# The first expert pair of a mixture-of-experts layer takes the form of the other three

## The chip, the cores and the metric

The kernel runs on one core of one Trainium2 chip, in one launch. The metric is the device time of that launch in microseconds (us); the median of a few runs counts. The profile is of one execution of its own, whose span is given beside it.

## The reference, cut to what matters

The program is one step of a small language model: an attention layer with a dense feed-forward part, then a state-space layer with a mixture of experts. There are 264 tokens, 256 of a prompt and 8 of samples. Only the last part, the mixture of experts, is touched:

```python
def moe(h, w_router, w_gate, w_up, w_down):
    probs = jax.nn.softmax((h @ w_router).astype(F32), axis=-1)
    top_p, top_i = lax.top_k(probs, TOP_K)              # TOP_K = 2 of N_EXPERTS = 8
    top_p = top_p / jnp.sum(top_p, axis=-1, keepdims=True)
    combine = jnp.sum(jax.nn.one_hot(top_i, N_EXPERTS, dtype=F32) * top_p[..., None], axis=-2)
    y = 0
    for e in range(N_EXPERTS):
        y = y + combine[..., e:e + 1] * swiglu(h, w_gate[e], w_up[e], w_down[e])
    return y
```

D_MODEL is 1024, an expert's hidden width is 2816, everything is float32. `setup_inputs(seed=0)` draws the inputs. Where the reference's own router is evaluated on these default inputs, the 528 choices of its 264 tokens fall on experts 0 to 7 like this: 104, 58, 93, 35, 49, 65, 69, 55.

## The kernel before

**Experts by pairs.** The router's counts are sorted on VectorE, but expert 0 is always put at rank 0 (its key gets 1e6 added), so that its weights can be fetched before the router has decided. Ranks 1 to 7 follow by falling count. Pair p joins the expert of rank p ("heavy") with that of rank 4+p ("light"). Each pair has a fixed room for tokens, whatever the counts are: pair 0 has 128 tokens of expert 0 (`CAPH`) and 64 of its light expert (`CAPL`), pairs 1 to 3 have 96 (`CAP2`) and 64.

**Rounds.** The whole of the four pairs stands in a loop `Fori(0, rounds)` on each engine, and each round reads all weights of all eight experts again. `rounds` is computed on the chip (lines 2438 to 2448): it is 1 if count 0 less 32 (`CAPH - CAP2`), count 1, and count 4 plus 32 (`CAP2 - CAPL`) are at most 96, else 2, or 3 for still greater ones (the numbers are ranks). Tokens beyond the room are taken in the next round.

**Pair 0** has a form of its own. Its columns are cut into `GROUPS` of 512 (the last of 256), and `first_steps()` sets the order: the heavy expert's gate, up and down products of a group with 128 tokens as one 128x128 load and 512 moving columns (lines 1515 and 1556), the light ones, a step behind, with 64 tokens in two column groups of the array (lines 1530 and 1568). Its heavy tokens are gathered by products with a 0/1 matrix `pick` (line 1424), its light ones and all of pair 1 by an indirect DMA from a copy `hrow` of the tokens in memory, turned on TensorE (lines 1433, 1451, 1452).

**Pairs 1 to 3** run `pair_gate_up`, `pair_turn` and `pair_down` over three `SUPER` groups of 1024, 1024 and 768 columns. Four 32-column groups of the array work side by side: three with the heavy expert's 96 tokens and one with 32 of the light ones (lines 1622 and 1672), then the light expert's other 32 tokens (lines 1634 and 1678). While pair p ends, `gather` brings pair p+1's tokens by products (line 1455), and `indices` its row numbers (line 1466).

**Weights** come in tiles of 1 MiB (768 KiB in the last SUPER group) through a ring of 12 slots (`MS`), all issued by SyncE (SP) in the order `MOE_TILES`. A slot is filled again when TensorE has counted `moe_used` up to its tile. The first 10 tiles (`AHEAD`), all of expert 0, are issued before the router is done; the rest from the loop (line 674). At the end of a round SP issues those first tiles again for a next round, each in `PIECES` = 8 pieces of 128 KiB through a small loop (line 680), or in 2 pieces only if no round follows (`piece_step`).

**End of a round.** `return_rows` adds the last pair's rows to the tokens by products (lines 1477 and 1483), `keep_rows` stores the sums on VectorE (line 2566). The first product of a next round (`gather_by_product`) waits for all of `keep_rows`.

Of the kernel before, what the change touches and what calls it, by code (L numbers as in the profile page):

```python
# [13 lines left out]
F32 = mybir.dt.float32  # L14
# [34 lines left out]
ROUNDS = -(-T // CAPH)  # L49
# [15 lines left out]
GROUPS = [(512 * g, min(512, FF - 512 * g)) for g in range(-(-FF // 512))]  # L65
NG = len(GROUPS)
GATHERS = 5 + 4 * (NP - 1)
ROWS_IN = 48
# [4 lines left out]
EVENTS = 2 * NG + 9 * (NP - 1)  # L73
COPIES = 2 * NG + 2 * NSG * (NP - 1)


FIRST = 8
RETURNS = (2, 0, 1)
KEPT = 7


def first_steps():


    return [(g if g < NG else None, g - 1 if g >= 1 else None) for g in range(NG + 1)]


def first_events():


    return [(who, g) for hg_, lg in first_steps() for who, g in (("heavy", hg_), ("light", lg)) if g is not None]


def moe_order():


    def gate_up(who, g):
        return [(0, who, kind, g, i) for kind in ("gate", "up") for i in range(GROUPS[g][1] // 256)]

    def down(who, g):  # L100
        return [(0, who, "down", g, i) for i in range(GROUPS[g][1] // 256)]

    order = []
    for hg_, lg in first_steps():
        if hg_ is not None:
            order += gate_up("heavy", hg_)
        if lg is not None:
            order += down("heavy", lg)
        if lg:
            order += down("light", lg - 1)  # L110
        if lg is not None:
            order += gate_up("light", lg)
    order += down("light", NG - 1)
# [16 lines left out]
AHEAD, PIECES = 10, 8  # L130
# [15 lines left out]
def moe_round(t):  # L146


    return 16 * (MT // MS) + (16 * (PIECES - 1) if t % MS < AHEAD else 0)
# [42 lines left out]
def build(nc, a, o):  # L192
# [5 lines left out]
    def sem(name):  # L198
# [154 lines left out]
    actH, sgH = actX[:, 0:512], actX[:, 512:D]  # L353
# [22 lines left out]
    twice = sb("twice", [P, 2, CAPL], c=c4)  # L376
# [3 lines left out]
    actL, sgL = actLx[:, 0:256], actLx[:, 256:512]  # L380
# [3 lines left out]
    turnL = turnB[:, :, :].rearrange("p (q u) t -> p q (u t)", q=2)  # L384
# [3 lines left out]
    hrow = nc.dram_tensor("hrow", [T, D], F32, kind="Internal").ap()  # L388
    hgrow = sb("hgrow", [P, 2, D], c=c4)
    rowix = [sb(f"rowix{i}", [P, 1], I32, c=c4) for i in range(2)]  # L390
# [5 lines left out]
    xs2 = hgrow[0:NB, 0, :]  # L396
# [27 lines left out]
      gathered index_done index_ready rows_out rows_gathered hg_ready ye_ready rows_added gates_copied moe_used  # L424
# [22 lines left out]
    first_packed = {kind: a[f"moe_first_{kind}"] for kind in ("gate", "up", "down")}  # L447
    md = a["moe_w_down"].rearrange("e (c p) n -> e p c n", p=P)
# [61 lines left out]
    def index_bank(p):  # L510

        return bank[7] if p < 2 else bank[0]
# [11 lines left out]
    def _(sp):  # L524
# [76 lines left out]
        def first_tile(tile):  # L601


            _, _, kind, g, i = tile
            f0, width = GROUPS[g]
            base = f0 * D + i * P * SLOT
            return first_packed[kind][base:base + P * SLOT].rearrange("(p n) -> p n", p=P)

        def packed_rows(kind, e, g, block):
# [4 lines left out]
            return packed[kind][ds(e - 1, 1), base:base + P * rows * width].rearrange("a (p c n) -> (a p) c n", p=P, c=rows)  # L614

        def moe_load(tile, e):

            p, who, kind, g, i = tile
            t = MOE_AT[tile]
            f0, width = SUPER[g] if p else GROUPS[g]  # L620
            if not p and who == "heavy":
                src = first_tile(tile)
                dst = moe_slot(t)[:, 0:src.shape[1]]
            elif kind == "down" and p:
                src = md_rows[ds(e - 1, 1), :, f0 // 256 + i, :].rearrange("a p n -> (a p) n")
                dst = moe_slot(t)
            elif kind == "down":
                c0_ = f0 // P + 2 * i
                src = md[ds(e - 1, 1), :, c0_:c0_ + 2, :].rearrange("a p c n -> (a p) c n")
                dst = moe_slot(t).rearrange("p (c n) -> p c n", c=2)  # L630
            elif p:
                src = packed_rows(kind, e, g, i // (PACK[g] // 2))
                src = src[:, i % (PACK[g] // 2) * 2:i % (PACK[g] // 2) * 2 + 2, :].rearrange("p c n -> p (c n)")
                dst = moe_slot(t)[:, 0:2 * width]
            else:
                rows = SLOT // width
                G0 = SUPER[g // 2][0]
                src = packed_rows(kind, e, g // 2, i // (PACK[g // 2] // rows))
                c0_ = i % (PACK[g // 2] // rows) * rows
                src = src[:, c0_:c0_ + rows, f0 - G0:f0 - G0 + width]  # L640
                dst = moe_slot(t).rearrange("p (c n) -> p c n", c=rows)
            sp.dma_start(dst, src).then_inc(moe_ready[t % MS], 16)

        def moe_piece(t, j):


            src = first_tile(MOE_TILES[t])
# [15 lines left out]
        sp.wait_ge(s["router_done"], 1)  # L663
        for t in range(FIRST, AHEAD):
            moe_load(MOE_TILES[t], 0)
        sp.wait_ge(s["router_done"], 5)
        rounds = sp.value_load(rnd[0:1, 0:1], min_val=1, max_val=ROUNDS)
        with sp.Fori(0, rounds) as r:
            for p in range(NP):
                expert = pair_ids(p)  # L670
                for tile in tiles_of(p):
                    if MOE_AT[tile] >= AHEAD:
                        sp.wait_ge(s["moe_used"], r * MT + (MOE_AT[tile] + 1))
# [16 lines left out]
    def _(g):  # L690
# [124 lines left out]
        def gather_rows(who, cap):  # L815
            g.indirect_dma_start(out=hgrow[0:cap, who, :], out_offset=None, in_=hrow[:, :],
                                 in_offset=bass.IndirectOffsetOnAxis(ap=rowix[who][0:cap, 0:1], axis=0)).then_inc(s["rows_gathered"], 16)

# [4 lines left out]
        with g.Fori(0, rounds) as r:  # L823
            for p in range(NP):
                n = r * NP + p
                if p == 0:
                    g.wait_ge(s["index_ready"], 2 * n + 2)
                    log(5 * n)
                    gather_rows(1, CAPL)
                if p < NP - 1:  # L830
                    g.wait_ge(s["index_ready"], 2 * n + 4)
                    log(5 * n + 1)
                    if p == 0:
                        gather_rows(0, P)
                        gather_rows(1, CAPL - CAPA)
# [3 lines left out]
                    add_rows(xrow[:, :], addix[p % 2][0], yeH, CAP2 if p else CAPH)  # L839
# [12 lines left out]
    def _(pe):  # L852
# [561 lines left out]
        def gather_by_product(r):  # L1414
# [1346 lines left out]
```

## Time and profile before

| what | us |
|---|---|
| median of 3 runs | 1588.38 |
| lowest, highest | 1583.31, 1594.08 |
| the profiled execution: time | 1581.58 |
| the profiled execution: span | 1580.0 |

The span is shown on the page in 40 slices of 39.5 us, with the busy share of each engine in tenths. TensorE (PE) is busy in nearly all of them. The share of the 16 DMA engines is 9 in the first slice and then again from slice 25 on, to the end: these are the experts' weights. The clock granted to TensorE is 0.978 of full speed over the whole span. A matmul of float32 stands in the records as two, so that a count of records is twice the count of products in the code. Times in the views count from the start of the span. "PEld" is the load of the stationary operand, "SPq" the queue of SyncE that issues DMAs.

### The profile page before, as it was taken

How to read it: one execution, taken by the hardware profiler on the slowest of the kernel's cores; microseconds unless marked ns; L12 is line 12 of the kernel's file. 1: busy time of each engine (PE TensorE's matmuls, PEld its weight loads, DVE VectorE, ACT ScalarE, POOL GpSimd, SP SyncE). 2: the span in 40 equal slices, each digit the busy share in tenths (PEclk: the TensorE clock that was granted, in tenths of full speed). 3: DMA queues.
4: the chain of work that ended last, by engine and by line, in shares of the span. 5: the costliest groups of instructions: out<-in, count | busy, mean ns of one | idle time of the engine just before them, and what ended most of it. 6: DMA issues, size and time to landing. Idle time of an engine off the chain costs nothing.

```text
span 1580.0 us, 24287 instructions
## 1 busy us (share of the span) xinstructions
PE 1494.8 (95%) x9928; PEld 885.9 (56%) x9928; DVE 370.3 (23%) x903; ACT 260.1 (16%) x586; POOL 111.2 (7%) x167
## 2 busy tenths in 40 slices
PE   6999877999999999999998999999999999998998
PEld 3544545788888878778785554553344234432342
DVE  2223431300000055634576100001000100011104
ACT  2122320200000022357503100000000000000001
POOL 1101550000000000000010100000000100010000
PEclk9999997999999999999999999999999999999999
DMA  9759987244334553472358899999999999999995
GB/s 379 306 214 392 365 289 240 107 162 160 122 105 146 197 189 120 155 263 94 147 211 349 288 348 379 392 408 401 421 417 419 405 420 417 420 404 419 418 418 220
DMA packets 104011, 463.22 MB, mean 293 GB/s; under 512 B 16110, under 2 KB 35339, under 8 KB 62261
## 3 DMA queue, kind: packets, MB, share of 16 engines
q1 hardware_dynamic: 91136, 420.49, 68.7%
q0 software_dynamic: 10256, 39.98, 7.3%
q8 instruction: 79, 1.29, 0.3%
q10 hardware_dynamic: 2512, 1.23, 0.3%
q14 instruction: 28, 0.23, 0.0%
HBM read 446.30 MB, written 15.55 MB: 292 GB/s over the span
## 4 chain that ended last, share of the span: by engine, by line
PE 76%; DMA 11%; DVE 5%; issue 4%; POOL 2%; ACT 1%; SPq 0%; POOLq 0%; DVEq 0%
PE bank L1622 11%; PE bank L1177 10%; PE bank L1147 8%; PE bank L1672 5%; PE bank L1191 5%; PE bank L1515 5%; DMA ring<-in_moe_w_up 4%; DMA ringx<-in_moe_w_up 3%; PE bank L1634 3%; PE bank L1225 3%; PE bank L1530 2%; PE bank L1556 2%; PE bank L890 2%; PE bank L924 2%; PE bank L977 2%
## 5 line engine op out<-in xcount | busy, mean ns | idle before, releaser
L1622 PE MATMUL bank<-ring,hg 128*32 128x512 f32 (+1 forms) x1456 | 208.5, 566 | 7.8 <-DMA ring<-in_moe_w_up 7.1
L1177 PE MATMUL bank<-hT,ring 128*128 128x264 f32 x704 | 156.9, 386 | 0.3 <-ACT hT L1725 0.3
L1622 PE MATMUL bank<-ringx,hg 128*32 128x512 f32 (+1 forms) x848 | 146.1, 568 | 3.8 <-DMA ring<-in_moe_w_up 2.8
L1177 PEld LDWEIGHTS bank<-hT,ring 128*128 128x128 f32 x704 | 133.7, 190 | 23.4 <-issue 0.6
L1622 PEld LDWEIGHTS bank<-ring,hg 128*32 128x32 f32 x1456 | 62.7, 111 | 110.3 <-issue 99.8
L1147 PE MATMUL bank<-hT,ring 128*128 128x264 f32 x512 | 118.7, 394 | 1.7 <-ACT hT L1725 1.3
L1147 PEld LDWEIGHTS bank<-hT,ring 128*128 128x128 f32 x512 | 99.1, 194 | 19.9 <-issue 2.1
L1672 PE MATMUL bank<-ring,turnH 128*32 128x512 f32 x768 | 92.6, 603 | 0.0
L1191 PE MATMUL bank<-actT,ring 128*128 128x264 f32 x352 | 79.1, 386 | 0.6 <-DVE actT L2210 0.6
L1515 PE MATMUL bank<-ring,hg 128*128 128x512 f32 (+1 forms) x192 | 78.0, 560 | 0.6 <-ACT hg L1940 0.6
L1622 PEld LDWEIGHTS bank<-ringx,hg 128*32 128x32 f32 x848 | 44.2, 112 | 59.6 <-issue 55.8
L1191 PEld LDWEIGHTS bank<-actT,ring 128*128 128x128 f32 x352 | 66.8, 190 | 12.4 <-DVE actT L2210 1.0
L2628 DVE TENSOR_TENSOR actX<-actX,bank 128x512 f32<-128x512 f32 (+1 forms) x18 | 10.8, 640 | 265.3 <-PE bank L1622 265.3
L1147 PE MATMUL bank<-sz,ring 128*128 128x264 f32 x256 | 60.1, 394 | 3.9 <-DVE sz L2367 3.9
L1225 PE MATMUL bank<-hT,ring 128*128 128x264 f32 x256 | 60.0, 390 | 0.0
L1147 PEld LDWEIGHTS bank<-sz,ring 128*128 128x128 f32 x256 | 49.6, 194 | 13.2 <-DVE sz L2367 4.3
L1672 PEld LDWEIGHTS bank<-ring,turnH 128*32 128x32 f32 x768 | 26.3, 111 | 54.7 <-issue 54.5
L1515 PEld LDWEIGHTS bank<-ring,hg 128*128 128x128 f32 x192 | 35.6, 190 | 36.7 <-issue 35.9
L1225 PEld LDWEIGHTS bank<-hT,ring 128*128 128x128 f32 x256 | 47.6, 190 | 8.9 <-issue 0.9
L1970 ACT ACTIVATE actX<-bank 128x512 f32<-128x512 f32 (+1 forms) x18 | 9.1, 559 | 263.6 <-PE bank L1622 263.6
L890 PE MATMUL bank<-ring,scT 128*32 128x512 f32 x384 | 50.6, 619 | 0.0
L813 POOL DMA_DIRECT2D index_log<-rnd x11 | 6.0, 548 | 545.1 <-DVE yeH L2526 290.4
(565 smaller groups left out, 1787.4 us busy)
## 6 DMA issues: line engine op xcount, KB each, us to landing
ring<-in_moe_w_down SPq DMA_DIRECT2D x53, 1024.0 KB, 17.1
ring<-in_w_ada SPq DMA_DIRECT2D x48, 1024.0 KB, 11.2
ring<-in_moe_w_up SPq DMA_DIRECT2D x40, 1024.0 KB, 16.1
ring<-in_moe_w_gate SPq DMA_DIRECT2D x32, 1024.0 KB, 17.0
ringx<-in_moe_w_gate SPq DMA_DIRECT2D x27, 1024.0 KB, 12.8
ringx<-in_moe_w_down SPq DMA_DIRECT2D x24, 1024.0 KB, 18.1
ring<-in_ssm_w_in SPq DMA_DIRECT2D x20, 1024.0 KB, 4.9
ringx<-in_moe_w_up SPq DMA_DIRECT2D x19, 1024.0 KB, 15.9
```

Source lines behind the costliest of these rows:

```text
L890: m = mm(b_[32 * v_:32 * v_ + 32, :], scT[:, k, :], ring[:, n % NS, 512 * v_:512 * (v_ + 1)], start=k == 0, stop=k == DC - 1, skip_group_c ...
L924: m = mm(out, slot8(n)[:, k, (m_ % 2) * P:(m_ % 2) * P + width], hT[:, k, :], start=k == 0, stop=k == DC - 1)
L977: m = mm(bank[h % 2][0:QK, 0:T], wqb[:, k, h * QK:(h + 1) * QK], projT[:, k, :], start=k == 0, stop=k == QC - 1)
L1147: m = mm(bank[n % 4][:, 0:T], w[:, k, (n % per_tile) * P:(n % per_tile + 1) * P], rhs[:, k, :], start=k == 0, stop=k == kc - 1)
L1177: m = mm(bank[2 * w + q][:, 0:T], slot8(tl)[:, k, q * P:(q + 1) * P], hT[:, k, :], start=k == 0, stop=k == DC - 1)
L1191: m = mm(bank[2 * (j % 2) + q][:, 0:T], slot8(tl)[:, kk, q * P:(q + 1) * P], actT[:, k0 + kk, :], start=k == 0 and kk == 0, stop=k == 3 an ...
L1225: m = mm(bank[n % 2][:, 0:T], slot8(tl)[:, k, (n % 2) * P:(n % 2 + 1) * P], hT[:, k, :], start=k == 0, stop=k == DC - 1)
L1515: m = mm(bank[kind == "up"][:, 0:width], hg[:, k, 0:CAPH], w[:, kk, :], start=k == 0, stop=k == DC - 1)
L1530: m = mm(bank[2][64 * v_:64 * v_ + 64, 256 * b_:256 * b_ + width // 2], hg[:, k, CAPH:CAPS], w[:, kk, v_], start=k == 0, stop=k == DC - 1, ...
L1622: m = mm(bank[2 * b_ + u][rows, 0:HALVES[g][u]], hg[:, k, rows], w[:, kk, 512 * u:512 * u + HALVES[g][u]], start=k == 0, stop=k == DC - 1, ...
L1634: m = mm(bank[7][32 * v_:32 * v_ + 32, 0:half], hg[:, k, CAPH:CAPH + CAPA], light[("gate", "up")[v_ // 2]][:, kk, 512 * (v_ % 2):512 * (v_ ...
L1672: m = mm(bank[4 + half][rows, :], turnH[:, 4 * u + q, rows], w[:, kk, 512 * half:512 * (half + 1)], start=first and kk == 0, stop=last and ...
```

## The change

Pair 0 runs the same code as the other pairs: 96 tokens of expert 0, three column groups of four, with 32 of its light tokens beside them. `GROUPS`, `first_steps` and everything built on them goes. The room for expert 0 is now `CAP2` = 96, and the rule for `rounds` is changed to that. Light tokens of pair 0 and all of pair 1 are gathered by products: the copy `hrow`, the indirect gathers and the index columns `rowix` go. The order of tiles is heavy gate, heavy up, light gate, light up from the start, so that `AHEAD` becomes the six tiles 0, 1, 4, 5, 8 and 9, and the number of tiles grows from 276 to 280 with the same bytes but for rounding. The weights of all experts are packed alike.

```diff
-ROUNDS = -(-T // CAPH)
+ROUNDS = -(-T // CAP2)
...
-AHEAD, PIECES = 10, 8
+PIECES = 8
+AHEAD = [t for t in range(MS) if MOE_TILES[t][1] == "heavy"]
...
+def slot_free(t):
+    return t + 1 if t >= MT % MS else t + 1 + MS - MT % MS
...
         sp.wait_ge(s["st_ready"], NB - 2)
-        for t in range(FIRST):
-            sp.wait_ge(s["units"], unit(WOUT + t))
+        for t in AHEAD:
+            if t < NS:
+                sp.wait_ge(s["units"], unit(WOUT + t))
+            else:
+                sp.wait_ge(s["router_done"], 1)
             moe_load(MOE_TILES[t], 0)
...
-            for t in range(AHEAD):
-                sp.wait_ge(s["moe_used"], r * MT + (MT + t + 1))
+            for t in AHEAD:
+                sp.wait_ge(s["moe_used"], r * MT + (MT + slot_free(t)))
                 moe_piece(t, 0)
                 with sp.Fori(1, PIECES, step) as j:
                     moe_piece(t, j)
...
-        for t, (t0, tn) in enumerate(TOKS):
-            g.wait_ge(s["rows_copied"], DC + 2 * t + 4)
-            g.dma_start(hrow[t0:t0 + tn, :], htok[0:tn, t, :]).then_inc(s["rows_out"], 16)
-        g.wait_ge(s["rows_out"], 64)
...
-        def gather_by_product(r):
+        def gather_first(r):
             pe.wait_ge(s["rows_kept"], r * KEPT + 1)
...
-                        m = mm(bank[i % 2][:, j * CAPS:j * CAPS + CAPH], htok[0:tn, t, c * P:(c + 1) * P], pick[0:tn, t, 0:CAPH],
+                        m = mm(bank[i % 2][:, j * CAPS:j * CAPS + CAP2], htok[0:tn, t, c * P:(c + 1) * P], pick[0:tn, t, 0:CAP2],
                                start=t == 0, stop=t == 2)
                 m.then_inc(s["gathered"], 1)
+            pe.wait_ge(s["pick_ready"], r * NP + 1)
             for c in range(DC):
-                m = pe.transpose(bank[2][:, c * CAPL:(c + 1) * CAPL], hgrow[0:CAPL, 1, c * P:(c + 1) * P], ident[0:CAPL, 0:CAPL])
+                for t, (t0, tn) in enumerate(TOKS):
+                    m = mm(bank[2][:, c * CAPL:(c + 1) * CAPL], htok[0:tn, t, c * P:(c + 1) * P], pick[0:tn, t, CAP2:CAP2 + CAPL],
+                           start=t == 0, stop=t == 2)
             m.then_inc(s["gathered"], 1)
...
-            gather_by_product(r)
-            pe.wait_ge(s["hg_ready"], r * GATHERS + 4)
-            for step, (hg_, lg) in enumerate(first_steps()):
...
-            for p in range(1, NP):
+            gather_first(r)
+            indices(r * NP, 0)
+
+            for p in range(NP):
                 n = r * NP + p
...
         for i in (1, 2):
-            ins = v.scalar_tensor_tensor(out=cmx[:, i:i + 1], in0=sorted_cnt[:, 0:1], scalar=float(i * (CAP2 - CAPH)), in1=sorted_cnt[:, 1:2],
-                                         op0=ALU.add, op1=ALU.max)
+            ins = v.tensor_tensor(cmx[:, i:i + 1], sorted_cnt[:, 0:1], sorted_cnt[:, 1:2], ALU.max)
         link(ins)
```

The lines behind this, which turn `cmx` into `rounds`, stay as they are:

```python
        for i in (1, 2):
            ins = v.scalar_tensor_tensor(out=cmx[:, i:i + 1], in0=sorted_cnt[:, NP:NP + 1], scalar=float(i * (CAP2 - CAPL)), in1=cmx[:, i:i + 1],
                                         op0=ALU.add, op1=ALU.max)
        link(ins)
        link(v.tensor_scalar(cmx[:, 0:1], cmx[:, 1:2], float(CAP2), 1.0, ALU.is_gt, ALU.add))
        link(v.scalar_tensor_tensor(out=cmx[:, 3:4], in0=cmx[:, 2:3], scalar=float(2 * CAP2), in1=cmx[:, 0:1], op0=ALU.is_gt, op1=ALU.add))
        v.tensor_copy(rnd[:], cmx[0:1, 3:4]).then_inc(s["router_done"], 1)
```

## Rows read from the trace of the kernel before

**Rows 1.** Windows by stage: pair 0, pairs 1 to 3, the end
```profile
core 0: us, PE busy (x) PEld busy (x) DVE busy (x) ACT busy (x) POOL busy (x), PEclk, DMA share, GB/s
869.70:1066.10 196.40, 194.63 (x893) 101.40 (x895) 17.17 (x63) 14.76 (x29) 11.34 (x14) 0.99 0.97 363
1066.10:1230.00 163.90, 162.47 (x1506) 59.84 (x1508) 12.89 (x41) 9.82 (x19) 3.73 (x4) 0.99 1.02 415
1230.00:1397.90 167.90, 162.80 (x1508) 62.33 (x1500) 16.23 (x39) 11.01 (x21) 4.77 (x5) 0.99 1.01 415
1397.90:1561.40 163.50, 153.79 (x1434) 52.81 (x1426) 23.36 (x44) 10.74 (x19) 6.03 (x7) 0.98 1.00 406
1561.40:1580.00 18.60, 11.58 (x50) 4.94 (x46) 11.73 (x17) 5.07 (x15) 0.00 (x0) 0.85 0.22 79
```
**Rows 2.** The page's costliest groups: the products of pairs 1 to 3
```profile
L1622 PE MATMUL bank<-ring,hg 128*32 128x512 f32 (+1 forms) x1456 | 208.5, 566 | 7.8 <-DMA ring<-in_moe_w_up 7.1
L1622 PE MATMUL bank<-ringx,hg 128*32 128x512 f32 (+1 forms) x848 | 146.1, 568 | 3.8 <-DMA ring<-in_moe_w_up 2.8
```
**Rows 3.** Timeline of VectorE where the counts become `rounds` and `pick`
```profile
867.05 0.22 DVE L2437 TENSOR_REDUCE sorted_cnt<-order 128x8 f32<-128x64 f32 x1
867.30 0.23 DVE L2439 SCALAR_TENSOR_TENSOR cmx<-sorted_cnt 128x1 f32<-128x1 f32 x2
868.21 0.14 DVE L2448 CAST rnd<-cmx 1x1 int32<-1x1 f32 x1
871.65 0.67 DVE L2476 TENSOR_SCALAR pick<-twice,slots 128x128 f32<-128x128 f32 x3
```
**Rows 4.** Chain that ended last, start of pair 0: start, us, what
```profile
869.72 8.52 PE bank L1424 x48
878.24 0.02 issue
878.26 0.39 ACT hg L1940
878.65 0.22 issue
878.87 13.99 PE bank L1515 x32
```
**Rows 5.** Timeline of TensorE: a gather at 160 columns, the indices of a later pair
```profile
1198.59 4.89 PE L1455 MATMUL bank<-pick,htok 128*128 128x160 f32 x24
1148.65 1.97 PE L1466 MATMUL bank<-tags,pick 128*96 128x3 f32 x18
```
**Rows 6.** Timeline of SP's queue: last early tiles, first tiles of a light expert
```profile
860.05 1.69 SPq L642 DMA_DIRECT2D ringx<-in_moe_first_down  x2
871.49 1.48 SPq L642 DMA_DIRECT2D ringx<-in_moe_w_gate  x2
```
**Rows 7.** DMA issues: xcount, KB each, median us from issue to landing
```profile
ring<-in_moe_w_down SPq DMA_DIRECT2D x53, 1024.0 KB, 17.1
ring<-in_ssm_w_in SPq DMA_DIRECT2D x20, 1024.0 KB, 4.9
```
**Rows 8.** Windows of 20 us in pair 2, columns as in group 1
```profile
1360.00:1380.00 20.00, 20.00 (x159) 8.68 (x151) 0.29 (x1) 1.47 (x3) 0.00 (x0) 1.00 1.02 422
```
**Rows 9.** Timeline: the last products, the end of `return_rows` and `keep_rows`
```profile
1557.05 3.64 PE L1672 MATMUL bank<-ringx,turnH 128*32 128x512 f32 x32 [0.32 <-DMA ringx<-in_moe_w_down]
1560.48 1.07 PE L1678 MATMUL bank<-ringx,turnB 128*32 128x512 f32 x8
1571.43 1.29 DVE L2566 TENSOR_TENSOR yout<-yout,bank 128x512 f32<-128x512 f32 x2 [0.98 <-PE bank L1483]
```
**Rows 10.** SP's issues in pieces at the round's end, and how they land
```profile
1556.16 2.40 SPq L649 DMA_DIRECT2D ring<-in_moe_first_up  x4
1558.84 2.64 SPq L649 DMA_DIRECT2D ringx<-in_moe_first_down  x4
L649 SPq DMA_DIRECT2D ringx<-in_moe_first_down x4: 347/350/711, 1558.8 to 1561.1; - x4
DMA to landing us min/median/max: 2.8/4.8/19.9
```
**Rows 11.** Bytes read from and written to memory, from the page
```profile
HBM read 446.30 MB, written 15.55 MB: 292 GB/s over the span
```

More of the change, by code:

```diff
@@ L72 @@
 HALVES = [(512, w - 512) for f0, w in SUPER]
-EVENTS = 2 * NG + 9 * (NP - 1)
-COPIES = 2 * NG + 2 * NSG * (NP - 1)
-FIRST = 8
+EVENTS = 9 * NP
+COPIES = 2 * NSG * NP
 RETURNS = (2, 0, 1)
 KEPT = 7
[L82 to L91, printed above, removed]
 def moe_order():
[L97 to L101, printed above, removed]
     order = []
[L104 to L113, printed above, removed]
     def down_pair(p, g):
         return [(p, who, "down", g, i) for i in range(SUPER[g][1] // 256) for who in ("heavy", "light")]
-    for p in range(1, NP):
+    for p in range(NP):
         for g in range(NSG):
@@ L613, in packed_rows, with moe_source @@
             base = f0 * D + block * P * rows * width
-            return packed[kind][ds(e - 1, 1), base:base + P * rows * width].rearrange("a (p c n) -> (a p) c n", p=P, c=rows)
+            return packed[kind][ds(e, 1), base:base + P * rows * width].rearrange("a (p c n) -> (a p) c n", p=P, c=rows)
+        def moe_source(tile, e):
+            _, _, kind, g, i = tile
+            if kind == "down":
+                return md_rows[ds(e, 1), :, SUPER[g][0] // 256 + i, :].rearrange("a p n -> (a p) n")
+            src = packed_rows(kind, e, g, i // (PACK[g] // 2))
+            return src[:, i % (PACK[g] // 2) * 2:i % (PACK[g] // 2) * 2 + 2, :].rearrange("p c n -> p (c n)")
         def moe_load(tile, e):
-            p, who, kind, g, i = tile
             t = MOE_AT[tile]
[L620 to L642, printed above, removed]
+            src = moe_source(tile, e)
+            sp.dma_start(moe_slot(t)[:, 0:src.shape[1]], src).then_inc(moe_ready[t % MS], 16)
         def moe_piece(t, j):
-            src = first_tile(MOE_TILES[t])
+            src = moe_source(MOE_TILES[t], 0)
             w = src.shape[1] // PIECES
@@ L1461, in indices @@
             pe.wait_ge(s["pick_ready"], n + 1)
[L1462 to L1463 removed]
+            for r0, r1, c0_, q in ((0, CAP2, 0, p), (CAP2, P, 0, NP + p), (0, P, 8, NP + p)):
                 for t, (t0, tn) in enumerate(TOKS):
@@ L1548, in heavy_down @@
-            def heavy_down(g):
-                pe.wait_ge(s["moe_copied"], turns_before("heavy", g) + 1)
-                if g == 0:
-                    pe.wait_ge(s["ye_ready"], 3 * n + 2)
-                for i in range(GROUPS[g][1] // 256):
-                    w = weights(0, "heavy", "down", g, i)
-                    for q in range(2):
-                        for half in range(2):
-                            m = mm(bank[4 + half][:, :], turnH[:, 2 * i + q, :], w[:, q, 512 * half:512 * (half + 1)],
-                                   start=g == 0 and i == 0 and q == 0, stop=g == NG - 1 and q == 1)
-                    m.then_inc(s["moe_used"], 1)
@@ L1560, in light_down @@
-            def light_down(g):
-                pe.wait_ge(s["moe_copied"], turns_before("light", g) + 1)
-                if g == 0:
-                    pe.wait_ge(s["ye_ready"], 3 * n + 3)
-                for i in range(GROUPS[g][1] // 256):
-                    w = weights(0, "light", "down", g, i)
-                    for q in range(2):
-                        for v_ in range(2):
-                            m = mm(bank[6][64 * v_:64 * v_ + 64, :], turnL[:, i, 64 * q:64 * q + 64], w[:, q, 512 * v_:512 * (v_ + 1)],
-                                   start=g == 0 and i == 0 and q == 0, stop=g == NG - 1 and q == 1, skip_group_check=True)
-                    m.then_inc(s["moe_used"], 1)
@@ L2496, in row_indices @@
                 v.wait_ge(s["rows_added"], rows_in_memory(r, 1))
-            v.tensor_scalar(rowix[0][:], ix[:, 0:1], -1.0, 0.0, ALU.add, ALU.max)
-            few = CAPA if p else CAPL
-            if p < 2:
-                v.tensor_scalar(rowix[1][0:few, :], ix[0:few, 8:9], -1.0, 0.0, ALU.add, ALU.max)
             ins = v.tensor_copy(slotw[u][:], ix[:, 0:16].rearrange("p (w c) -> p w c", c=8)[:, :, 0:3])
@@ L2520, in heavy_slot_rows @@
         def heavy_slot_rows(r, p):
-            v.wait_ge(s["moe_used"], r * MT + moe_done(p, "heavy", "down", (NSG if p else NG) - 1))
+            v.wait_ge(s["moe_used"], r * MT + moe_done(p, "heavy", "down", NSG - 1))
             v.wait_ge(s["rows_added"], rows_in_memory(r, p))
```

273 lines of the change are left out of this document (56 added, 217 removed).

## The prediction

> **What bounds the kernel now.** I read the windows by stage first [rows 1]. From 869.7 us on, everything is the experts. In pair 0 TensorE is busy 194.6 of 196.4 us while the DMA engines move 363 GB/s: TensorE is the bound. In pairs 1 to 3 both are at their limit: TensorE is busy 162.5 of 163.9, 162.8 of 167.9 and 153.8 of 163.5 us (pair 3 gathers nothing), and the DMA share is 1.00 to 1.02 at 406 to 415 GB/s. So a pair in the wide form costs about 164 us whichever way one looks, and one in the old form 196.
>
> The second thing to read is a count. Line 1622 makes 1152 products in three pairs, which is 2304 records; the page has 1456 + 848 = 2304 [rows 2]. The loop over rounds has run exactly once. This sets what the time is made of: one round is 691.7 us (869.7 to 1561.4) of 1580, so whatever touches the number of rounds outweighs everything else in the diff.
>
> **The rule for rounds.** The counts of the default inputs are 104 for expert 0, and 93, 69, 65, 58, 55, 49, 35 for the others by rank. Before: max(104 - 32, 93, 58 + 32) = 93, not over 96, one round. After: max(104, 93, 58 + 32) = 104, over 96, and max(104, 93, 58 + 64) = 122, not over 192: two rounds. Eight tokens of expert 0 have no room in the first round, and for these the second reads all eight experts again, since no product or load in the loop depends on how many tokens a slot holds.
>
> Did the chip see these inputs? The counts themselves do not stand in a trace; the instructions that sort them take the same 0.22 us whatever they hold [rows 3]. But the single round [rows 2] is a test of them: it needs count 0 up to 128, rank 1 up to 96 and rank 4 up to 64. I evaluated the router on seeds 0 to 5 under both of the random generator's modes: of 12 draws only two pass, the default one and one more (49 tokens for expert 0). That speaks strongly for the default inputs, and the margin of 8 tokens is no matter of rounding.
>
> **The first round's start.** Heavy tokens are still gathered by 24 products, and 24 more now follow for the light ones. At 128 moving columns 48 records took 8.52 us [rows 4]; at 160 columns 24 records took 4.89 us [rows 5]. Going by columns down to 64 would give about 6.5 us, going by the number of products 8.5; I take 8.5 for both parts and keep 2 us each as the bound. The light part's `pick` was ready at 872.3 us [rows 3]; nine VectorE operations in place of three add perhaps 1.5 us, still before TensorE is through the heavy part at 878.2. The indices of pair 0, 18 records at 1.9 us [rows 5], now stand ahead of the first weights, and the copy of the light tokens lies beside them. First expert product: 869.7 + 8.5 + 8.5 + 1.9 = 888.6 us (before 878.9).
>
> Loads: only six tiles can be fetched early, because the light expert isn't known before. SP gets past the router at 871.5 [rows 6]; six tiles of 1.05 MB at 422 GB/s [rows 8] are 15 us, so the ring is full at about 888. This costs nothing; were TensorE ready at 880, it would cost 8 us. The `hrow` copies and gathers that go were beside other work: nothing. Waits taken away on SP, POOL and ACT end no earlier than what follows them.
>
> **The first round's pairs.** By TensorE: 3 x 163.9 + 153.8 = 645.5 us (the first pair now as the second, with a gather for the next). By DMA: eight experts are 8 x 3 x 1024 x 2816 x 4 B = 277 MB; less 12.6 MB in the ring at the start, at 415 GB/s, 637 us, plus the last tiles' products of 4.3 us [rows 9]: 641. As these two are so close, they will take turns in holding the other up, as they did before: the old pairs 1 to 3 took 495.3 us where TensorE alone needs 481.6. From above, the sum of the old pairs with a second "pair 1" is 495.3 + 163.9 = 659.2. I take 652, the middle. The round's products end at 888.6 + 652 = 1540.6 us (before 1561.4): the wide form alone is worth some 21 us.
>
> The Trainium skill's page "DMA: Bandwidth & Descriptors", section "Specifications", gives a fabric ceiling of 435 GB/s and a limit of about 358 GB/s for the memory of one core. The rate of 422 GB/s in a window agrees with the first and not with the second. An estimate by the second would be 774 us for a round's 277 MB, which the measured stages exclude, and by the first 637 us.
>
> **Between the rounds.** What was hidden at the end of a single round is on the path now. `return_rows` and `keep_rows`: from the last product at 1561.4 to VectorE's last sum at 1572.7 is 11.3 us [rows 9], then `gather_first` 17 and `indices` 1.9: TensorE could start 30.2 us after the last product. The loads: `slot_free` makes SP wait with tile 0 until the last but one block of the last down product is used, 4.3 us before that end, so nothing of round 2 is fetched earlier. Then come six tiles in eight pieces each, 48 issues. In the trace four issues begin 0.75 us apart (2.24 us over three, the last being 0.35 long) [rows 10], so 48 take 36 us and end 32 us after the last product. Tiles 2 and 3 of the light expert are queued behind them on SP, and TensorE needs them for its first product: 1 MiB lands in 4.9 us on a quiet queue [rows 7], the second one 2.5 us later, together 39 us after the last product. Lower bound 30.2 (pieces at 0.35 us each), upper bound 45.
>
> **The second round's pairs** start with about 8 of 12 tiles there, not 12: (277 - 8.4) / 415 is 647 us plus 4.3. I take 655, between 645.5 and 659.2.
>
> **The end**: 18.6 us in the span as before and 1.6 outside it [rows 1]; two pieces of each of six early tiles instead of ten change nothing there.
>
> **Sum** against the profiled execution of 1581.58: 1540.6 + 39 + 655 + 18.6 + 1.6 = 2254.8 us. The median of the runs is 6.8 us above the profiled one (1588.38), so about 2260 for a median.
>
> **The rivals.**
> *One round after all* (the other side). If the chip's inputs give expert 0 at most 96 tokens, the sum ends at 1540.6 + 20.2 = 1560.8, or about 1567 as a median (1555 to 1583), 1.3% faster. It decides at 96 against 97 tokens. For it: another draw with 49 tokens also fits the single round. Against it: it would have to be other inputs than the reference draws by default.
> *The pieces come one after another.* If each of the 48 waited for its landing, 2.8 us at least [rows 10], the first product of round 2 would come at 134 + 3 us behind the last instead of 39, and the median would be about 2355. Against it: the pieces in the trace are issued 0.75 us apart, before the one ahead of them can have landed.
> *Round 2 is cheap*, because it has eight tokens. The products' shapes are fixed and all weights are loaded; nothing in the loop skips. It would take a skip that the code doesn't have, so it only stands here to be named.
> *The clock or the rate falls in the longer run.* The granted clock is 0.98 to 0.99 in all four pairs [rows 1], with no trend; a loss of 3% over both rounds would be 39 us, a median near 2300.
>
> **Chances.** Two rounds as summed 0.87; serial pieces 0.02; lower clock or rate 0.06; one round 0.05. Range: from below, TensorE alone without a wait, 888.6 + 645.5 + 30.2 + 645.5 + 20.2 = 2230; from above 888.6 + 659.2 + 45 + 659.2 + 20.2 = 2272, plus the spread of the runs (the highest is 12.5 above the profiled one, on 1.4 times the length 18) = 2290. I give 2235 to 2295. A measurement of this kernel can tell about 1% (16 us) from no change. One round would be mostly faster by over 1%, in part within 1%: faster 0.03, same 0.02, slower 0.95.
>
> **What would show each step.** Line 1622's successor has 1152 / 3 x 4 x 2 x 2 = 6144 records for two rounds and 3072 for one. Memory reads rise from 446 [rows 11] to about 723 MB. The first expert product stands near 889 us, the first round's last down product near 1541, with no gap over a few us between. Then TensorE is without expert products for 39 us, and its last wait there is for a light expert's tile, behind 48 short issues on SP; if that wait is missing and the gap is 30 us, the pieces are cheaper than I think. If pairs 0 to 3 take over 660 us, the DMA rate was lower than in the trace; if there is one round, my reading of the inputs was wrong, and with it everything else.

## The result

The changed kernel takes 2300.42 us (median of 4 runs, 2295.34 to 2302.65), the kernel before 1585.97 us beside it (1583.31 to 1594.08). The ratio is 1.450, with a 95% interval of 1.445 to 1.455: slower by 714 us. The forecast was 2260 with a range of 2235 to 2295. The direction and the cause were right. The size was 40 us short, and the median lies 5 us above the range.

The page of the changed kernel, its products and its traffic. They answer to [rows 2] and [rows 11]:

```profile
span 2297.9 us, 39979 instructions
...
HBM read 722.24 MB, written 16.30 MB: 321 GB/s over the span
...
L1440 PE MATMUL bank<-ring,hg 128*32 128x512 f32 (+1 forms) x4160 | 547.7, 566 | 27.5 <-DMA ring<-in_moe_w_up 18.4
...
L1440 PE MATMUL bank<-ringx,hg 128*32 128x512 f32 (+1 forms) x1984 | 307.3, 562 | 10.4 <-DMA ringx<-in_moe_w_up 6.7
```

Line 1440 (1622 before) has 4160 + 1984 = 6144 records, which is four pairs in two rounds; one round would be 3072. The reads from memory rose by 276 MB, the weights of eight experts once more.

The windows by stage, as in [rows 1]: the four pairs of round 1, the gap, the four pairs of round 2, the end.

```profile
core 0: us, PE busy (x) PEld busy (x) DVE busy (x) ACT busy (x) POOL busy (x), PEclk, DMA share, GB/s
906.70:1070.50 163.80, 162.36 (x1505) 58.95 (x1508) 12.73 (x43) 9.81 (x19) 0.52 (x1) 0.99 0.97 398
1070.50:1236.70 166.20, 161.75 (x1504) 60.41 (x1500) 17.24 (x47) 10.99 (x21) 4.88 (x5) 1.00 1.01 416
1236.70:1405.90 169.20, 161.50 (x1508) 62.81 (x1500) 16.15 (x38) 10.99 (x21) 4.79 (x5) 1.00 1.01 415
1405.90:1569.50 163.60, 153.84 (x1434) 54.35 (x1426) 24.20 (x50) 10.53 (x18) 6.07 (x7) 0.98 0.97 394
1569.50:1614.70 45.20, 38.63 (x144) 27.46 (x141) 10.56 (x31) 3.20 (x6) 0.00 (x0) 0.64 0.56 182
1614.70:1781.20 166.50, 165.06 (x1504) 60.25 (x1508) 9.95 (x25) 9.82 (x19) 0.53 (x1) 0.97 1.01 414
1781.20:1945.50 164.30, 161.12 (x1504) 61.57 (x1500) 17.16 (x47) 11.00 (x21) 4.80 (x5) 1.00 1.02 416
1945.50:2115.50 170.00, 161.74 (x1508) 62.44 (x1504) 16.19 (x39) 10.99 (x21) 4.76 (x5) 1.00 1.02 416
2115.50:2279.40 163.90, 154.08 (x1434) 55.16 (x1426) 24.29 (x51) 10.73 (x19) 6.04 (x7) 0.98 0.97 395
2279.40:2297.90 18.50, 10.56 (x41) 4.04 (x38) 11.60 (x17) 5.07 (x15) 0.00 (x0) 0.85 0.30 103
```

Pair 0 takes 163.8 us where it took 196.4. All the rest of the story starts at the fifth row: behind pair 3 there are 45.2 us without an expert's product, and then everything again. The second round and its gap are 2279.4 - 1569.5 = 709.9 us, 99% of the 714 us.

TensorE's timeline ahead of round 1, and in the gap, with SP's queue beside it:

```profile
875.37 3.48 PE L802 MATMUL bank<-cst 128*128 128x512 f32 x4 [0.71 <-ACT yout L1549]
878.75 11.59 PE L1359 MATMUL bank<-pick,htok 128*128 128x96 f32 x48
890.27 13.35 PE L1365 MATMUL bank<-pick,htok 128*128 128x64 f32 x48
903.55 3.17 PE L1391 MATMUL bank<-tags,pick 128*96 128x3 f32 x18
906.65 8.64 PE L1440 MATMUL bank<-ring,hg 128*32 128x512 f32 x64
...
1580.82 13.06 PE L1359 MATMUL bank<-pick,htok 128*128 128x96 f32 x48 [1.37 <-DVE yout L2355]
1593.81 13.35 PE L1365 MATMUL bank<-pick,htok 128*128 128x64 f32 x48
1607.09 3.17 PE L1391 MATMUL bank<-tags,pick 128*96 128x3 f32 x18
1614.70 5.72 PE L1440 MATMUL bank<-ring,hg 128*32 128x512 f32 x28 [4.45 <-DMA ring<-in_moe_w_up]
```
```profile
1564.03 6.11 SPq L598 DMA_DIRECT2D ring<-in_moe_w_gate  x8
...
1595.88 7.17 SPq L598 DMA_DIRECT2D ringx<-in_moe_w_up  x8
1606.90 0.36 SPq L591 DMA_DIRECT2D ring<-in_moe_w_gate  x1
1607.46 0.35 SPq L591 DMA_DIRECT2D ring<-in_moe_w_up  x1
```

The gathers have 24 products each, like the one in [rows 4], but take 11.6 and 13.4 us and not 8.5. In the gap SP is busy with the 48 pieces from 1564.0 to 1603.1. The light expert's first tile is issued 3.8 us later; the loop has to come round in between. TensorE's last wait, 4.45 us, is for the second of these tiles.

### The profile page after: what moved, and what is told of

It is laid out like the page before. It is cut to its first block, busy times and chain, and to the rows that moved or that the text cites. A ratio compares the mean times of both kernels' runs of the same rounds, so it can differ in the third digit from the quotient of the medians.

```text
span 2297.9 us, 39979 instructions
## 1 busy us (share of the span) xinstructions
PE 2174.6 (95%) x16719; PEld 1138.1 (50%) x16719; DVE 453.7 (20%) x1092; ACT 305.9 (13%) x670; POOL 122.2 (5%) x178
## 4 chain that ended last, share of the span: by engine, by line
PE 45%; DMA 14%; SPq 2%; issue 1%; DVE 1%; ACT 0%; DVEq 0%; POOLq 0%
PE bank L1440 18%; PE bank L1490 12%; DMA ring<-in_moe_w_up 8%; DMA ringx<-in_moe_w_up 6%; PE bank L1452 5%; PE bank L1496 3%; PE bank L1380 3%; DMA ring<-in_moe_w_down 1%; PE bank L1467 1%; SPq L598 1%; PE bank L1391 1%; PE bank L1365 1%; PE bank L1470 1%; PE bank L1359 0%; SPq L591 0%
## 5 line engine op out<-in xcount | busy, mean ns | idle before, releaser
L1440 PE MATMUL bank<-ring,hg 128*32 128x512 f32 (+1 forms) x4160 | 547.7, 566 | 27.5 <-DMA ring<-in_moe_w_up 18.4
L1440 PEld LDWEIGHTS bank<-ring,hg 128*32 128x32 f32 x4160 | 169.8, 111 | 308.9 <-issue 281.9
L1440 PE MATMUL bank<-ringx,hg 128*32 128x512 f32 (+1 forms) x1984 | 307.3, 562 | 10.4 <-DMA ringx<-in_moe_w_up 6.7
L1490 PE MATMUL bank<-ring,turnH 128*32 128x512 f32 x1792 | 212.6, 597 | 1.1 <-DMA ring<-in_moe_w_down 1.1
L1440 PEld LDWEIGHTS bank<-ringx,hg 128*32 128x32 f32 x1984 | 95.8, 110 | 145.3 <-issue 141.4
L1112 PEld LDWEIGHTS bank<-hT,ring 128*128 128x128 f32 x704 | 133.7, 190 | 23.4 <-issue 0.6
L1452 PE MATMUL bank<-ring,hg 128*32 128x512 f32 (+1 forms) x1088 | 132.1, 554 | 0.0
L1490 PEld LDWEIGHTS bank<-ring,turnH 128*32 128x32 f32 x1792 | 62.7, 110 | 126.1 <-issue 125.1
L1490 PE MATMUL bank<-ringx,turnH 128*32 128x512 f32 x1024 | 120.3, 593 | 0.0
L1082 PEld LDWEIGHTS bank<-hT,ring 128*128 128x128 f32 x512 | 98.9, 194 | 19.8 <-issue 2.1
L1452 PEld LDWEIGHTS bank<-ring,hg 128*32 128x32 f32 x1088 | 40.4, 110 | 66.8 <-issue 60.5
L1490 PEld LDWEIGHTS bank<-ringx,turnH 128*32 128x32 f32 x1024 | 33.8, 110 | 71.8 <-issue 71.8
L1496 PE MATMUL bank<-ring,turnB 128*32 128x512 f32 x448 | 66.8, 592 | 0.0
## 6 DMA issues: line engine op xcount, KB each, us to landing
ringx<-in_moe_w_down SPq DMA_DIRECT2D x64, 1024.0 KB, 17.6
ringx<-in_moe_w_up SPq DMA_DIRECT2D x41, 1024.0 KB, 18.6
```

What stands on the lines that cost most here:

```text
L1082: m = mm(bank[n % 4][:, 0:T], w[:, k, (n % per_tile) * P:(n % per_tile + 1) * P], rhs[:, k, :], start=k == 0, stop=k == kc - 1)
L1112: m = mm(bank[2 * w + q][:, 0:T], slot8(tl)[:, k, q * P:(q + 1) * P], hT[:, k, :], start=k == 0, stop=k == DC - 1)
L1440: m = mm(bank[2 * b_ + u][rows, 0:HALVES[g][u]], hg[:, k, rows], w[:, kk, 512 * u:512 * u + HALVES[g][u]], start=k == 0, stop=k == DC - 1, ...
L1452: m = mm(bank[7][32 * v_:32 * v_ + 32, 0:half], hg[:, k, CAPH:CAPH + CAPA], light[("gate", "up")[v_ // 2]][:, kk, 512 * (v_ % 2):512 * (v_ ...
L1490: m = mm(bank[4 + half][rows, :], turnH[:, 4 * u + q, rows], w[:, kk, 512 * half:512 * (half + 1)], start=first and kk == 0, stop=last and ...
L1496: m = mm(bank[6][rows, :], turnB[:, q, 32 * u:32 * u + 32], light[:, kk, 512 * half:512 * (half + 1)], start=first, stop=last, skip_group_ ...
```

## The experiments

The stages below are read from each kernel's timeline of TensorE: from the router's first product to the first expert product; the four pairs of round 1; the gap; the four pairs of round 2. Times in us; ends of products are modelled, so that they differ by 0.1 from the windows above.

| kernel | router at | to first expert product | round 1 | gap | round 2 |
|---|---|---|---|---|---|
| before | 853.0 | 25.8 | 682.7 | | |
| changed | 861.2 | 45.5 | 662.9 | 45.1 | 664.7 |
| e1_one_round | 857.3 | 43.0 | 664.9 | | |
| e3_one_gather | 856.8 | 41.7 | 664.7 | 44.3 | 665.0 |
| e4_two_pieces | 859.4 | 45.0 | 665.4 | 39.4 | 664.9 |
| e5_half_loads | 859.7 | 42.8 | 644.6 | 45.9 | 644.0 |
| e6_gather_pieces_early | 853.0 | 41.7 | 664.9 | 23.0 | 663.3 |
| e7_filled_gather | 852.9 | 42.0 | 665.6 | 53.2 | 665.1 |
| e8_one_round_best | 853.3 | 34.0 | 662.2 | | |

### Is it the count, and which count

```diff
-        link(v.tensor_scalar(cmx[:, 0:1], cmx[:, 1:2], float(CAP2), 1.0, ALU.is_gt, ALU.add))
+        link(v.tensor_scalar(cmx[:, 0:1], cmx[:, 1:2], 103.0, 1.0, ALU.is_gt, ALU.add))
```

The second kernel has 104.0 there.

> The changed kernel with its threshold for a second round at 103 instead of 96. The chip thus says itself whether its largest count among the heavy experts is over 103. If expert 0 holds 104 tokens, as the reference's router says, two rounds run: about 2300. If the count is anything from 97 to 103, one round, about 1588, with tokens left out.

> The same with the threshold at 104; 8 tokens of expert 0 then get nothing from it. If expert 0 holds exactly 104 tokens, one round runs: about 1588. If it holds 105 or more, two rounds, 2300. Two neighbouring numbers that give 2300 and 1588 pin the count.

Measured in one run each: 2294.63 and 1582.13 us, beside 1583.67 for the kernel before. The products of the second (the page) are those of one round, 2080 + 992 = 3072 records:

```profile
L1440 PE MATMUL bank<-ring,hg 128*32 128x512 f32 (+1 forms) x2080 | 276.0, 565 | 9.4 <-DMA ring<-in_moe_w_up 4.9
L1440 PE MATMUL bank<-ringx,hg 128*32 128x512 f32 (+1 forms) x992 | 154.7, 566 | 5.3 <-DMA ringx<-in_moe_w_up 2.8
```

One step of the threshold moves 712 us. The greatest of the three terms on the chip is exactly the reference's 104, and it is expert 0's: the kernel before needs only one round, so each of the other two terms is at most 96 in it. The prediction had to infer the default inputs; the one count on which the rounds hang is now measured, the other seven are not.

### One round of the new form

```diff
-        link(v.tensor_scalar(cmx[:, 0:1], cmx[:, 1:2], float(CAP2), 1.0, ALU.is_gt, ALU.add))
+        link(v.tensor_scalar(cmx[:, 0:1], cmx[:, 1:2], float(CAPH), 1.0, ALU.is_gt, ALU.add))
```

> The changed kernel with the threshold for a second round at 128 instead of 96, so that one round runs and the 8 tokens of expert 0 beyond its room get nothing from it: that part is left out. If the second round is the whole of the loss, the time falls by the second block of four pairs and the gap before it (2279.4 - 1569.5 = 709.9 us of the changed kernel's trace) to about 1590, equal to the kernel before within 1%. Rival, my prediction's own step: the wide form is worth 21 us in one round, so about 1567.

Measured: 1588.07 us against 1585.83, ratio 1.0022 (1.0004 to 1.0039). So the second round is all of the loss but 2 us, and the 21 us that I had given to the wide form are not there. The table shows where they went. The pairs do save 17.8 us (682.7 to 664.9), where my sum had some 30, and 17.1 us is given back ahead of them (25.85 to 42.97), where my sum had 9.8.

### Two rounds of the old form

The same line in the kernel before, with `float(CAPL)`, a threshold of 64; the largest of its three terms is 93, by the reference's counts.

> The kernel before with the threshold at 64 instead of 96, so that it runs a second round in which no token is left. If rounds alone explain the loss, this unchanged code takes 1586 + 692 for the pairs + a gap. In the gap ten tiles go out in 80 pieces at 0.82 us (39.4 us for 48 in the changed kernel's trace), about 66 us, less what lies before the last product: about 2335, slower than the changed kernel's 2300. Rival, that the new form of pair 0 itself costs something large: this one stays well below 2300.

Measured: 2314.38 us, ratio 1.4597 (1.4571 to 1.4623). With nothing changed but its threshold, the kernel before becomes slower than the changed kernel, by 14 us, as soon as it makes two rounds. The expected 2335 was 21 us too high. The first product of its second round came 24.8 us after the last of its first (1567.8 to 1592.6) where 2335 would leave 57, since the first heavy tiles were there. The pieces went on until 1619.4 and delayed only what followed: the second round's pairs took 700.0 us against 683.4 for the first.

### The gap: gathers and pieces

e3 gathers pair 0's tokens as `gather` does for the others:

```diff
         def gather_first(r):
             pe.wait_ge(s["rows_kept"], r * KEPT + 1)
-            for i in range(4):
...
+            gather(r, 0)
...
-            f(hg[:, :, CAP2:CAP2 + CAPL], bank[2][:, :].rearrange("p (c t) -> p c t", c=DC), ACT.Copy).then_inc(s["hg_ready"], 1)
```

> The changed kernel, but the tokens of pair 0 are gathered like those of the others, 96 + 64 columns in 24 products instead of 24 of 96 and 24 of 64 columns. In the changed kernel's trace these took 11.5 + 13.3 us in round 1 and 13.0 + 13.3 in round 2, with the granted clock near 0.5. At full clock 24 products of 160 columns took 9.8 us, at half perhaps 15. Theory: round 1 starts 9 to 12 us earlier (a wait of 3 us for the later pick against it), round 2 gains only the 4.4 us that TensorE did not already wait for its tile in the gap, if at all; in all 9 to 14 us less, about 2288. Rival: the clock is low whatever is gathered and the loads of round 1 then bind; no gain.

e4 changes one number:

```diff
-PIECES = 8
+PIECES = 2
```

> The changed kernel with 2 pieces of 512 KiB instead of 8 of 128 KiB for each early tile of a next round. Theory: SP's 48 issues of 0.82 us each held back the light expert's tile 3 and with it the first product of round 2; with 12 issues SP is through in 10 us, the gap is then TensorE's own (return_rows, gathers, indices, 40.8 us), 4.4 us shorter, and 4 more tiles are in the ring at its end, which may take 2 to 3 us of waits off round 2. About 5 us less, 2295. Rival: the pieces cost nothing beyond that and the time is the same. At the very end 5.5 MB more are loaded for no use, beside the tail.

Measured: 2293.64 (ratio 1.4473, 1.4449 to 1.4497) and 2291.64 us (1.4449, 1.4425 to 1.4474): 7 us less than the changed kernel, where 9 to 14 were expected, and 9 us less, where 5 were. In e3 the start gained 3.8 us and not 9 to 12, since the one gather took 17.6 us at a granted clock of 0.50 and not the 15 that I had put for it. The gap hardly moved, 44.3 us. Its timeline of TensorE there shows why:

```profile
1574.49 9.71 PE L1365 MATMUL bank<-pick,htok 128*128 128x160 f32 x48 [1.45 <-DVE yout L2338]
1584.12 2.17 PE L1376 MATMUL bank<-tags,pick 128*96 128x3 f32 x18
1607.45 4.50 PE L1425 MATMUL bank<-ring,hg 128*32 128x512 f32 x20 [21.16 <-DMA ring<-in_moe_w_up]
```

The gather takes 9.7 us in place of 26.4, and TensorE then waits 21.2 us for the light expert's tile behind the pieces. In e4, with SP through its 12 pieces at 1570.8, the gap is 39.4 us of TensorE's own work, its gathers and indices at a granted clock of 0.55, and no wait for a tile. Each limit hides the other, which the two together should show. e6 has both edits, and issues the early tiles in the order in which their slots come free:

```diff
-            for t in AHEAD:
-                sp.wait_ge(s["moe_used"], r * MT + (MT + slot_free(t)))
+            for t in AHEAD[2:] + AHEAD[:2]:
+                sp.wait_ge(s["moe_used"], r * MT + (MT + (t - 3 if t >= 4 else t + 9)))
```

> The changed kernel with the gather of 24 products, 2 pieces, and the early tiles issued in the order of their slots' release (tiles 4, 5, 8, 9 first, each as soon as its own slot is free). With one gather alone TensorE waited 21.2 us in the gap for tile 3 behind 48 pieces, with 2 pieces alone the gap was 39.4 us of gathers at the low clock. Theory: these two limits hide each other, and together the gap falls from 45.2 us to TensorE's own 11.3 + 9.7 + 2.2 = 23 to 25; with 4 us less before round 1 and a fuller ring in round 2, about 2272. Rival, they add only singly: 2300 - 7 - 9 = 2284.

Measured: 2274.72 us, ratio 1.4351 (1.4304 to 1.4398). The gap is 23.0 us, at the full clock, with no tile waited for:

```profile
1559.60:1582.60 23.00, 20.81 (x93) 11.49 (x94) 7.67 (x13) 3.03 (x5) 0.00 (x0) 0.99 0.92 370
```

This is the best form of two rounds found here, and still 691 us behind the kernel before. The third edit, the earlier issue, was not run by itself, and why the gather ran at the full clock here is not known; the 16.4 us between the gaps of e4 and e6 come from the other gather at a higher clock.

### What bounds a round of wide pairs

e5 leaves out half of each weight tile behind the first twelve; the products stay as they are:

```diff
-            sp.dma_start(moe_slot(t)[:, 0:src.shape[1]], src).then_inc(moe_ready[t % MS], 16)
+            w = src.shape[1] if t < MS else src.shape[1] // 2
+            sp.dma_start(moe_slot(t)[:, 0:w], src[:, 0:w]).then_inc(moe_ready[t % MS], 16)
```

> The changed kernel, each weight tile after the first 12 loaded with only its first half (4 KiB of 8 KiB per partition); the products run over the whole slot, so the experts' results are left wrong and only the time counts. If the DMA rate is what keeps four wide pairs at 663 to 665 us where TensorE alone needs 3 x 163.9 + 153.8 = 645.5, the waits for tiles vanish and both blocks come to about 646, in all some 36 us less, 2262 to 2266. Rival, TensorE's own work is the 664 us (clock, evictions): the time stays at 2295 or more.

Measured: 2257.32 us, ratio 1.4239 (1.4192 to 1.4285), 43 us less than the changed kernel, where 36 were expected. By the profiles 39 of them lie in the two rounds. The windows of the two rounds, of e5 first and then of the changed kernel:

```profile
902.60:1547.20 644.60, 638.85 (x5935) 229.49 (x5934) 70.35 (x174) 42.33 (x79) 16.25 (x18) 0.99 0.66 212
1593.10:2237.10 644.00, 638.25 (x5934) 229.43 (x5934) 67.62 (x156) 42.53 (x80) 16.14 (x18) 0.99 0.68 218
```
```profile
906.70:1569.50 662.80, 639.44 (x5935) 236.52 (x5934) 70.31 (x173) 42.33 (x79) 16.26 (x18) 0.99 0.99 406
1614.70:2279.40 664.70, 642.01 (x5934) 239.42 (x5934) 67.59 (x156) 42.55 (x80) 16.14 (x18) 0.99 1.00 410
```

With the DMA share at 0.66 the same products take 644.6 and 644.0 us: TensorE's own time, which the prediction had put at 645.5. Loaded in full, the DMA share is 0.99 to 1.00 and a round takes 18 to 21 us more. TensorE's waits for tiles come to 17.6 us in the first round of the changed kernel, 4.4 in the gap and 17.0 in the second round; in e5 one of 5.3 us is left, in the gap. So supply binds the wide form.

### The clock in the gathers

e7 puts eight products of 512 columns between the narrow ones:

```diff
                 m.then_inc(s["gathered"], 1)
+                keep_clock(bank[6], 1)
             pe.wait_ge(s["pick_ready"], r * NP + 1)
             for c in range(DC):
+                if c % 2 == 0:
+                    keep_clock(bank[6], 1)
```

> The changed kernel with one product of 512 columns put after each 6 of the narrow gather products, 8 in all per round (0.86 us each at full clock). In all kernels of the new form the granted clock was 0.5 through the gathers before round 1 (27.3 us of it in the changed kernel). If the narrow products themselves are what lets the clock fall, the wider ones between them hold it at 1.0: gathers and fill take about 24 us instead of 24.8, the indices 1.9 instead of 3.1 and the first products 1.6 us less; 3 us less before round 1, little in round 2 where tile 3 binds. About 2297. Rival, the clock falls for another reason: 8 fills at half clock add 14 us before round 1, about 2312.

Measured: 2298.78 us (ratio 1.4473, 1.4411 to 1.4534), which can't be told from the changed kernel. That it is near the 2297 expected is luck: the start did become 3.5 us shorter, as reckoned, but the gap became 8.1 us longer, and in this profile the router's first product comes 8.2 us earlier than in the changed kernel's. Its timeline has both outcomes in one execution, round 1 and then round 2:

```profile
873.49 1.97 PE L1359 MATMUL bank<-pick,htok 128*128 128x96 f32 x12
...
885.69 1.86 PE L1368 MATMUL bank<-pick,htok 128*128 128x64 f32 x12
...
1580.15 3.44 PE L1359 MATMUL bank<-pick,htok 128*128 128x96 f32 x12
...
1597.37 3.23 PE L1368 MATMUL bank<-pick,htok 128*128 128x64 f32 x12
```

The same instructions ran at 1.97 and 1.86 us ahead of round 1 and at 3.44 and 3.23 ahead of round 2, where the gap grew to 53.2 us. So the fill doesn't hold the clock by itself, and that the narrow products alone bring it down isn't shown either. e8 puts six wide products ahead of a single gather, in one round:

```diff
             pe.wait_ge(s["rows_kept"], r * KEPT + 1)
+            keep_clock(bank[6], 6)
             gather(r, 0)
```

> One round only, as in e1_one_round (the 8 tokens of expert 0 over its room are left out), with the gather of 24 products and 6 products of 512 columns ahead of it, in the time in which TensorE waited for the light pick (5.1 us in e3_one_gather). Theory: the clock stays high, the gather takes 9.7 us and the indices 1.9 instead of 17.6 and 3.1, so the first expert product comes 33 us after the router's first product instead of 42 to 43: 1588 - 10 = 1578, 0.5% under the kernel before. Rival, the DMA engines bind the whole block of pairs, so what is won at the start is waited for later: 1586 to 1588.

Measured: 1572.49 us, ratio 0.9926 (0.9900 to 0.9952).

```profile
867.75 8.27 PE L802 MATMUL bank<-cst 128*128 128x512 f32 x14
875.86 9.61 PE L1366 MATMUL bank<-pick,htok 128*128 128x160 f32 x48
885.39 1.97 PE L1377 MATMUL bank<-tags,pick 128*96 128x3 f32 x18
887.29 7.07 PE L1426 MATMUL bank<-ring,hg 128*32 128x512 f32 x64
```

At the full clock the gather takes 9.6 us (17.6 in e3) and the first expert product comes 34.0 us after the router's first. The 7.7 us won there against e3 were not waited for again in the pairs (662.2 us). This is what the new form could give if the tokens fitted: 0.7% or 12 us under the kernel before, of the 21 us that I had forecast for it. The stages say the same: 20.5 us less in the pairs and 8.1 more ahead of them. With 104 tokens for expert 0 it leaves eight of them out.

No version beat the kernel before with all tokens. One with a room of 128 in the wide form wasn't tried. For its 32 further tokens it would need the products of lines 1634 and 1678 a second time. In pair 1 of the kernel before these are 8 blocks of 1.72 us, 4 of about 1.3 us and 11 of 0.86 us, some 28 us on TensorE. By this estimate pair 0 would take about 192 us, close to the old form's 196.4.

## Why the prediction was right on the rounds and 40 us short on the time

**The rounds: right.** A few VectorE operations of 0.14 to 0.23 us decide [rows 3], and the two sides of the comparison were taken from the code and from the reference's counts. e9 and e10 confirm the count itself, e1 and e2 that form and rounds are separate: the new form in one round costs what the old one does, the old form in two rounds costs 14 us more than the new one.

**The sum was 44.7 us short** (2254.8 against 2299.5 for the profiled execution). By its own steps:

| step | predicted | measured | off |
|---|---|---|---|
| first expert product | 888.6 | 906.7 | +18.1 |
| pairs of round 1 | 652 | 662.8 | +10.8 |
| gap | 39 | 45.2 | +6.2 |
| pairs of round 2 | 655 | 664.7 | +9.7 |
| end, in the span | 18.6 | 18.5 | -0.1 |

**What failed** are two terms: the supply of weights in the rounds of pairs, taken as 652 and 655 us with 659.2 as the upper bound of each, and the gathers ahead of them, taken at the full clock. The range itself was worked out from such bounds, 2272 us and 18 for the spread of the runs. The execution came out 27 us above the 2272: 18.1 at the first expert product, 9.1 in the two rounds, 0.2 in the gap.

*First expert product.* 8.1 us of the 18.1 lie ahead of the router. Its first product stands at 853.0 in the profile of before and at 861.2 in that of the changed kernel. Over all twelve profiles it scatters from 852.3 to 861.2, and e6, e7 and e8, all of the new form, have it at 852.9 to 853.3. So this is the spread of executions and not the change; the profile that I worked from stood at its low end. The other 10 us are mostly the clock. I took 8.5 us per 24 products from a row at full clock [rows 4] and treated it as a property of the product. The two gathers took 11.6 and 13.4 us, and the indices 3.2 and not 1.9. From 878.8 to 906.7 TensorE was busy without a break, and the granted clock was 0.56:

```profile
878.80:906.70 27.90, 27.90 (x119) 23.73 (x122) 5.04 (x22) 3.20 (x6) 1.98 (x2) 0.56 0.61 245
```

At the full clock the term would have held. Ahead of round 1 of e7 the eight groups of six narrow products, which are the same two gathers, take 15.4 us together, against 17 in my sum.

*The pairs.* By the weights alone I had 637 us at 415 GB/s and 4.3 for the last tiles, 641; by TensorE alone 645.5. I took 652, the middle between 645.5 and 659.2, and the measured rounds are above the upper bound. The rate in the middle of a round was as I had read it; what I had wrong were the two ends and the bytes. The last stretch before round 1, then the first, the middle and the last stretch of round 1:

```profile
900.00:906.70 6.70, 6.70 (x36) 6.01 (x39) 0.00 (x0) 1.88 (x2) 0.00 (x0) 0.50 0.00 1
906.70:923.30 16.60, 16.60 (x145) 4.49 (x148) 2.79 (x18) 0.00 (x0) 0.00 (x0) 0.91 0.60 202
923.30:1552.90 629.60, 606.50 (x5650) 227.18 (x5646) 63.19 (x151) 40.66 (x77) 16.26 (x18) 0.99 1.01 416
1552.90:1569.50 16.60, 16.34 (x152) 4.85 (x144) 4.33 (x4) 1.67 (x2) 0.00 (x0) 1.00 0.58 224
```

With the ring full, nothing moves until TensorE has given back a slot: SP issues the next tile at 911.9, 5.2 us after the first product. At the end no tile is left to issue: from 1556 to 1564 the last ones come in at 213 GB/s, with the DMA engines half busy (why isn't shown), and the pieces of the next round start only at 1564.0. The two end stretches together move 7.1 MB in 33.2 us, which at 416 GB/s would be 17 us: 16 us lost where I had 4.3. And the round moves 268.9 MB, not the 264.4 of its weights, because returned rows, copies of tokens, instructions and the first pieces for the next round go the same way. 268.9 MB at 416 GB/s are 646 us, and with the 16 us that is the measured 662.8. Round 2 has no idle start and fewer tiles in the ring, 272.7 MB in all, and comes to 664.7.

The upper bound had the same fault: it gave one more pair 163.9 us, TensorE's time, while its 69.2 MB need 166 us at 416 GB/s. e5 turned the supply from an argument into a measurement. The prediction's own sign, that a round over 660 us would mean a lower DMA rate than in the trace, does not hold as it stands: the averages of 406 and 410 GB/s are lower, the rate of the long middle is not.

*The gap.* The pieces took 39.0 us for 48, 0.82 us from one to the next, against my 0.75 from four issues [rows 10]; and between the last piece and the first tile of the light expert there are 3.8 us, which I hadn't priced. TensorE's own side was 40.8 us and not 30.2, by the clock again, but hidden: the pieces bound, as forecast.

**The rivals.** Serial pieces: refuted by 0.82 us per piece. Round 2 cheap because it holds eight tokens: refuted, 664.7 us against 662.8 for the first. One round: it would have given 1588 and not 1567. A lower clock or rate: its "median near 2300" is what was measured, but by luck. It spoke of a loss of 3% all through both rounds, and the pairs ran at a granted clock of 0.97 to 1.00; the clock fell only in the gathers, where it cost 10 us on the path.

**The rate.** The Trainium skill's page "DMA: Bandwidth & Descriptors", section "Specifications", gives about 358 GB/s as the memory's limit for one core. Both rounds ran at 406 and 410 GB/s for over 660 us each; with no second core at work the lower figure does not bind here, as the prediction had read from a single window.

## What to carry to other kernels

Look for the data that decide how often a loop runs before looking at how fast one pass is: a room that is 8 tokens too small cost 45%, and a single number of the code against a single number of the inputs told it in advance. Where two engines are within 3% of each other over a stage, a change that relieves one gives at most what the other leaves, and the stages at its ends, hidden before, have to be priced anew. Price the start and the end of a stream of loads apart from its rate: here the rate was right, and 16 us of the first round lay in the ends. Two limits that lie over each other, here the pieces and the gathers, look small when taken away one at a time (5.7 and 0.8 us of the gap) and are worth 22 us together (with the early tiles issued sooner).

## What the runs showed of the hardware that I had not expected

The granted clock stood at 0.50 to 0.56, mostly its lower level of 1.2 GHz, through 17.6 to 38.9 us (e3 and e7) in which TensorE was busy without a break, with products of 64 to 160 moving columns and their loads (in e7 with eight of 512 between them). The Trainium skill's page "TensorE: Matmul & The Clock Gate", section "Loop structure matters more than you think", says that matmuls that follow each other back to back stay warm; the trace disagrees, with 27.90 us busy in 27.90 us at 0.56. What tips it is open: the same 128-column gather ran in 8.5 us in the kernel before and in 12.9 us in the second round of e2, the same 160-column gather in 17.6 us ahead of round 1 of e3 and in 9.7 us ahead of its round 2. In e8 it was fast directly behind six wide products, in e3's round 1 slow behind a wait of 5.1 us; but the four records of 512 columns ahead of that wait had already taken 3.46 us, against 1.98 in the kernel before, and e7's round 2 was slow with no wait over 1.4 us ahead of it.

A DMA issue in SP's small loop costs 0.82 us although the instruction itself lasts 0.34, so 48 pieces of 128 KiB leave the queue at about 160 GB/s where whole tiles run at 415. From the last piece to the first tile of the next round SP's queue is empty for 3.8 to 4.1 us in the kernels with 8 pieces and for 6.5 us in e4 and e6, which have 2; what fills this time isn't shown.

The three VectorE operations that make expert 0's `pick` end 2.10 us after they start in the changed kernel, with 96 columns, and 0.66 us in the kernel before, with 128. With the clock high TensorE waits 1.4 us for them (e4, e7). The cause is open.
